# The second block's first half: the context as a thread of its own, woven between the latents' stages, its weights streamed twice

## The reference, cut to what matters

```
for i in (0, 1):                       # layer 0: MLA, layer 1: neighbourhood attention (NA)
    mod   = silu(c)     @ ada_w[i] + ada_b[i]     # shifts, scales, gates of the latents
    mod_c = silu(c_ctx) @ ada_w[i] + ada_b[i]     # and of the context
    h, hc = x * (1 + sc1) + sh1, ctx * (1 + csc1) + csh1
    y, yc = mixer(h, hc)               # latents attend to context and latents, the context to itself
    x   = layer_norm(alpha * x + g1 * y)
    ctx = layer_norm(alpha * ctx + cg1 * yc)             # layer 0 only
    x   = layer_norm(alpha * x + g2 * mlp(x * (1 + sc2) + sh2))
    ctx = layer_norm(alpha * ctx + cg2 * mlp(ctx * (1 + csc2) + csh2))   # layer 0 only
```

## Time and profile before

| | |
|---|---|
| median of the runs | 3009.98 us (3008.04 to 3012.18) |
| profiled execution, span | 3008.3 us |
| PE busy | 2883.5 us, 96% |
| PEld busy | 2401.1 us, 80% |
| DVE busy | 1953.4 us, 65% |
| ACT busy | 1152.3 us, 38% |
| POOL busy | 316.4 us, 11% |
| HBM read | 408.67 MB, 136 GB/s over the span |
| mean granted TensorE clock | 0.974 |

### The profile page before, as it was taken

How to read it: one execution, slowest core, us unless ns; L and a number is a source line. 1 busy time by engine, 2 the same in 40 slices (tenths; PEclk the granted TensorE clock), 3 DMA queues, 4 the chain that set the end, 5 groups by cost and what they waited for, 6 DMA issues and landing times.

```text
span 3008.3 us, 39317 instructions
## 1 busy us (share of the span) xinstructions
PE 2883.5 (96%) x15758; PEld 2401.1 (80%) x15758; DVE 1953.4 (65%) x3295; ACT 1152.3 (38%) x1901; POOL 316.4 (11%) x380
## 2 busy tenths in 40 slices
PE   7999999988999999999999899999999999998898
PEld 6888897546888888888887799976788888876898
DVE  7788855645688856778655765554566765457654
ACT  4222244443422224222254654434352223535553
POOL 0000011322100001000011120210230001200100
PEclk8999999979999999999999999999999999999999
DMA  6666522101455535555332245421134442343453
GB/s 239 222 218 227 186 86 88 42 28 42 154 204 202 203 105 175 198 201 209 114 124 73 68 161 183 147 84 36 64 118 161 169 147 92 92 103 79 130 186 119
DMA packets 126004, 412.27 MB, mean 137 GB/s; under 512 B 25296, under 2 KB 27472, under 8 KB 125312
## 3 DMA queue, kind: packets, MB, share of 16 engines
q1 hardware_dynamic: 110272, 353.14, 35.0%
q0 software_dynamic: 15552, 56.63, 5.3%
HBM read 408.67 MB, written 1.05 MB: 136 GB/s over the span
## 4 chain that ended last, share of the span: by engine, by line
PE 84%; DVE 6%; ACT 5%; issue 1%; DMA 1%; POOL 1%; SPq 0%; ACTq 0%; POOLq 0%; DVEq 0%
PE bank L2409 26%; PE bank L2410 25%; PE bank L2411 25%; PE bank L2678 2%; DVE sb_split_low L1829 1%; ACT sb_split_high L1415 1%; POOL sb_temp L1288 1%; DVE sb_h_low L1916 1%; DMA sb_na_raw<-na_rpb 1%; PE bank L2639 1%; DVE sb_temp L1910 1%; PE bank L2826 1%; PE bank L2761 0%; PE bank L2612 0%; DMA sb_raw<-weights 0%
## 5 line engine op out<-in xcount | busy, mean ns | idle before, releaser
L2409 PE MATMUL bank<-sb_h_high,sb_split_high 128*128 128x256 f32 (+1 forms) x3040 | 1050.3, 346 | 40.4 <-DVE sb_h_low L1924 18.7
L2410 PE MATMUL bank<-sb_h_low,sb_split_high 128*128 128x256 f32 (+1 forms) x3040 | 1030.2, 339 | 0.0
L2411 PE MATMUL bank<-sb_h_high,sb_split_low 128*128 128x256 f32 (+1 forms) x3040 | 1029.9, 339 | 0.0
L1829 DVE TENSOR_TENSOR sb_split_low<-sb_raw,sb_split_high 128x1024 fp32r<-128x1024 f32 x515 | 632.0, 1234 | 229.9 <-ACT sb_split_high L1415 227.2
L2409 PEld LDWEIGHTS bank<-sb_h_high,sb_split_high 128*128 128x128 f32 x3040 | 581.6, 191 | 128.6 <-DVE sb_h_low L1924 19.9
L1415 ACT ACTIVATE sb_split_high<-sb_raw 128x1024 fp32r<-128x1024 f32 x515 | 536.5, 1051 | 322.4 <-DMA sb_raw<-weights 322.2
L2411 PEld LDWEIGHTS bank<-sb_h_high,sb_split_low 128*128 128x128 f32 x3040 | 582.3, 192 | 64.7
L2410 PEld LDWEIGHTS bank<-sb_h_low,sb_split_high 128*128 128x128 f32 x3040 | 582.9, 192 | 63.7 <-issue 0.5
L1843 DVE CUSTOM_DVE_ANT_0 sb_temp<-sb_ada_ffn,sb_cond_ffn 128x1024 bf16<-128x1024 f32 x396 | 465.9, 1220 | 16.9 <-DMA sb_ada_ffn<-ada 8.5
L2032 DVE SCALAR_TENSOR_TENSOR sb_x_res<-bank,sb_gates,sb_x_res 128x256 f32<-128x256 f32 x320 | 145.1, 480 | 231.0 <-PE bank L2411 224.2
L2409 PE MATMUL bank<-sb_hidden_high_ffn,sb_split_high 128*128 128x512 f32 (+1 forms) x830 | 279.6, 337 | 0.0
(11 more groups left out here) (291 smaller groups left out, 3046.1 us busy)
## 6 DMA issues: line engine op xcount, KB each, us to landing
sb_raw<-weights SPq DMA_DIRECT2D x515, 512.0 KB, 3.3
sb_ada_ffn<-ada SPq DMA_DIRECT2D x114, 512.0 KB, 4.4
sb_ada_ffn<-ada POOLq DMA_DIRECT2D x90, 512.0 KB, 3.7
sb_ada_mlp<-ada POOLq DMA_DIRECT2D x18, 512.0 KB, 3.5
sb_ada_mlp<-ada SPq DMA_DIRECT2D x18, 512.0 KB, 4.3
sb_cond_ffn<-cond SPq DMA_DIRECT2D x3, 1024.0 KB, 5.1
sb_na_raw<-na_rpb SPq DMA_DIRECT2D x32, 96.0 KB, 6.0
sb_x_res<-tokens SPq DMA_DIRECT2D x4, 512.0 KB, 7.4
```

What stands on the lines that cost most here:

```text
L1829: do.tensor_tensor(m.low[i][:, :], m.raw[i][:, :], m.high[i][:, :].bitcast(F32), ALU.subtract).then_inc(*dve.mark("split_low", s))
L2409: do.matmul(out, ah, bh, start=start and j == 0, stop=False)
L2410: do.matmul(out, ah, bl, start=False, stop=False)
L2411: last = do.matmul(out, al, bh, start=False, stop=stop and j == len(terms) - 1)
```

## The change

The context's layer 0 and its keys and values for layer 1 get steps, slabs and signals of their own, with a `c` ahead of the name (`cmla_down`, `cmla_out`, `cmlp0`, `cna_k`, `cna_v0`, ...). The latents' ones become `LAT_PART`. The 105 slabs that both need are laid in the stream twice, each where it is used (`PLACE`, worked out from the order of the `done` steps). All the products of this half have 256 columns, but those of `mla_v` and `na_v`, whose moving side is the weights.

- `beside_ffn11`: the context's whole attention (down-projection, front, 8 units, out-projection, layer norm `cln00`) in banks 0 to 3, the pieces of the latents' `ffn11` between them in banks 4 and 5; the rest of `ffn11` follows.
- `beside_mla`: the latents' final norm, MLA and layer norm `ln00`, with the 64 pieces of the context's perceptron `cmlp0` between them; the rest of `cmlp0` follows.
- `beside_mlp0`: the latents' `mlp0` with the 36 rows of modulation, the context's second norm `cln01` woven into its first eight pieces and the tiles `cp10` into its last five; then the latents' norm `ln01` with the pieces of `cna_k` and `cna_v` between its groups.
- `na_steps` begins with the latents' `na_k` and `na_q` in turns of one slab each; five slabs of each lie beside the units, two in a turn, then `na_v1`.
- The warm matmuls of these norms are left out (those of `n12` and of the last half of `odd_out` stay). `ffn11` is cut in chunks of 8, 7, 7 instead of 22. The scores of layer 1 are two matmuls of 256 keys. SBUF is laid out anew; scales, gates and two temporaries exist twice.

The diff, cut to its core:

```diff
-          ("mla_down", 7), ("mla_uk0", 1), ("mla_v0", 1), ("mla_pe", 2), ("mla_uq0", 2),
-          ("mla_uq2", 2), ("mla_uk1", 1), ("mla_v1", 1), ("mla_out", 8), ("mlp0", 64),
-          ("na_k", 8), ("na_q", 5), ("na_v0", 4), ("na_q5", 3), ("na_v1", 4), ("na_out", 8), ("mlp1", 64)]
+          *((c + name, n) for c in ("c", "") for name, n in (
+              ("mla_down", 7), ("mla_uk0", 1), ("mla_v0", 1), ("mla_pe", 2), ("mla_uq0", 4), ("mla_uk1", 1), ("mla_v1", 1),
+              ("mla_out", 8), ("mlp0", 64), ("na_k", 8), ("na_v0", 4), ("na_v1", 4))),
+          ("na_q", 8), ("na_out", 8), ("mlp1", 64)]
...
-    "mlp0": ("relu2", 204, 36, BOTH),
+    "cmlp0": ("relu2", 0, 0, CTX_PART),
+    "mlp0": ("relu2", 204, 36, LAT_PART),
...
+def filled(groups, fill, n=1):
+
+    for group in groups:
+        yield from group
+        for _ in range(n):
+            if fill:
+                yield from fill.pop(0)
...
+def mla_front(p, ring, fill):
+
+    kv, q = of(p, "mla_kv"), of(p, "mla_q")
     square, add = (lambda tag, k: ("small_square", tag, k)), (lambda tag, k: ("small_sum", tag, k))
...
+    groups = [[square(kv, 0), square(kv, 1)],
+              [add(kv, 0), add(kv, 1), square(q, 0), square(q, 1), ("mean", kv, p)],
+              [add(q, 0), add(q, 1), square(q, 2), square(q, 3)],
+              [("mla_norm", kv, 0), ("mla_norm", kv, 1)] + [("rope", "mla_k", 0, 7)] * (p == LAT_PART),
+              [add(q, 2), add(q, 3), ("mean", q, p)]]
+    yield from filled(groups, fill)
...
+def mla_units(p):
+
+    return list(pair_turns(of(p, "mla"), 8, 2))
...
+def beside_ffn11():
+
+    ring = Ring(0, 6)
+    tiles = plain_tiles("cp00", 0)
+    early = in_groups([t for t in tiles if t[0] == "plain" or t[2] < 4], (1,) * 11)
+    late = [t for t in tiles if t[0] != "plain" and t[2] >= 4]
+    first, *rest = [out_piece("odd_out", k, 1, LAT_PART, ring) for k in range(DT)]
+    yield from weave([kept_warm(first, 8), *rest], early)
+    down = [fm_piece("cmla_down", j, CTX_PART, ring) for j in range(7)]
+    norm = ada_norm_groups("n12", 1)
+    yield from norm[0]
+    yield from late
+    yield from down[0]
+    yield from weave(norm[1:], down[1:4])
+    yield "gates", "ffn11"
+    _, body, _ = ffn_pieces("ffn11", Ring(4, 2), 0, 0)
+    ring = Ring(0, 4)
+    yield from filled([[], *down[4:]], body)
+    yield from mla_front(CTX_PART, ring, body)
+    ring = Ring(4, 2)
+    own = mla_own(CTX_PART, Ring(0, 4))
+    yield from flat(own)
+    yield from beside(mla_units(CTX_PART), body)
+    yield "gates", "cmla_out"
+    ring = Ring(0, 4)
+    outs = [out_piece("cmla_out", k, half, CTX_PART, ring) for half in (0, 1) for k in range(DT)]
+    yield from weave(outs, [body.pop(0) for _ in range(8)])
+    yield "scales", "cp01"
+    yield from filled(layer_and_plain_groups("cln00", "cp01", 0), body)
+    yield from flat(body)
...
+def beside_mla():
+
+    _, fill, _ = ffn_pieces("cmlp0", Ring(4, 2), 0, 0)
+    ring = Ring(0, 4)
+    yield "gates", "cmlp0"
+    yield "scales", "p00"
+    yield from filled([[("sum", "final", 1), ("mean", "final", 1)], [("rstd_spread", "final", 1), ("final_norm",)]], fill)
+    yield from filled(in_groups(plain_tiles("p00", 1), (4,)), fill)
+    yield from flat(fm_piece("mla_down", j, LAT_PART, ring) for j in range(7))
+    yield "gates", "mla_out"
+    yield from mla_front(LAT_PART, ring, fill)
+    own = mla_own(LAT_PART, Ring(0, 4))
+    yield from flat(own)
+    yield from beside(mla_units(LAT_PART), fill)
+    ring = Ring(0, 4)
+    outs = [out_piece("mla_out", k, half, LAT_PART, ring) for half in (0, 1) for k in range(DT)]
+    yield "cond", "mlp0", 1
+    yield from weave(outs, [fill.pop(0) for _ in range(4)])
+    yield "scales", "p01"
+    yield from filled(layer_and_plain_groups("ln00", "p01", 1), fill, 2)
+    yield "cond_silu", "mlp0"
+    yield from flat(fill)
...
+def beside_mlp0():
+
+    yield "gates", "mlp0"
+    ring = Ring(0, 6)
+    _, body, _ = ffn_pieces("mlp0", ring, 0, 0)
+    pieces = list(ada_pieces("mlp0", body))
+    yield from weave(pieces[:8], [[], [], *layer_norm_groups("cln01", 0)])
+    yield from flat(pieces[8:-5])
+    yield "scales", "cp10"
+    yield "scales", "p10"
+    yield from weave(pieces[-5:], in_groups(plain_tiles("cp10", 0), (5, 5, 5, 5)))
+    ring = Ring(0, 6)
+    yield "na_bv",
+    yield "na_rpb", 0
+    names = [fm_piece("cna_k", j, CTX_PART, ring) for j in range(8)] + [piece for g in (0, 1) for piece in tm_pieces(f"cna_v{g}", ring)]
+    yield from filled(layer_and_plain_groups("ln01", "p10", 1), names, 2)
+    yield "gates", "na_out"
+    yield from flat(names)
...
         if k == 0:
             return
+        if tag == "cln01":
+            pool.wait_ge("turned", ("mla", 7, 1))
```

More of the change, by code:

```diff
@@ L958, in schedule, with places @@
+def places():
+    order_of = [step[1] for step in order() if step[0] == "done"]
+    assert sorted(order_of) == list(range(N_SLABS))
+    at = [0] * N_SLABS
+    for i, s in enumerate(order_of):
+        at[s] = i
+    return at
+PLACE = places()
 def schedule():
@@ L2504, in small_sum @@
         pe.wait_ge("squared", (tag, k))
-        do.matmul(m.bank[bank][:, 0:n], m.C("ones"), m.squares[k % 2][:, 0:n], start=k == 0, stop=k == tiles - 1).then_inc(
+        do.matmul(m.bank[bank][:, 0:NC_TOK], m.C("ones"), m.squares[k % 2][:, cols], start=k == 0, stop=k == tiles - 1).then_inc(
             *pe.mark("summed", (tag, k)))
@@ L2541, in out @@
         if halves:
[L2542 removed]
+            s, first = PLACE[SLAB0[name] + 4 * half + k // 2], halves[half]
             free(bank)
@@ L2827, in mla_scores @@
-        for c in range(2):
-            bank, rows = (2 * u + c) % 3, slice(HD * c, HD * c + HD)
-            do.matmul(m.bank[bank][:, 0:n], big[rows, MLA_QPE + pair, qs], big[rows, MLA_KPE, 0:n], start=False, stop=True).then_inc(
-                *pe.mark("scored", ("mla", u, c)))
-            read[bank] = "exped", ("mla", u, c)
+        pair_of_scores("mla", u)
     def na_scores(u):
```

572 lines of the change are left out of this document (321 added, 251 removed), and 2 rows, old and new, of the table GATES.

## The result

The changed kernel takes 3091.06 us (median of 4 runs, 3089.63 to 3095.13) against 3010.28 us before (4 runs beside it). The ratio is 1.0269, with a 95% interval of 1.0257 to 1.0281: 81 us slower. The forecast was 3005 us, range 2978 to 3032. It had the wrong sign, and the time lies 59 us above the range.

What follows compares the result with a forecast made beforehand. TensorE, busy 2883.5 of 3008.3 us, was taken as the bound, so only its waits or slowness could be won. Terms 7 + 2 - 47 + 5 - 8 + 32 + 4 = -5 gave 3005 us, range 2978 to 3032.

Steps and rivals of the forecast that it cites:

- the -47 around the norms: Around the norms: TensorE's 73 us of gaps would be filled except 26 us of remaining waits, winning 47 us.
- the -8 of the second attention: Second attention: ten slabs' products of na_k and na_q as filler would cut TensorE's idle time, winning 8 us.
- The width, +7: Products split from 512 columns into two of 256 would cost 7 us more in all.
- "VectorE needs ... a step of 4.11": mlp0, +32: Latents' mlp0: VectorE's steps, up to 4.11 us, outlast TensorE's slabs, so it takes 212 us, not 180: 32 us more.
- Rival B: Latents' mlp0: VectorE's load decides, TensorE waits 50 us instead of 32; 3030 us in all, slower; chance 0.20.
- the 36 stay: Latents' mlp0: the 36 modulation rows VectorE works out remain beside it though the context's half leaves; within the +32 us.
- "Attention", first one, +5: First attention: waits from head pairs sharing bank 6, now four pairs each for context and latents, would add 5 us.
- two together in a turn: Second attention: a slab each of na_k and na_q beside one turn gives 5.6 us of filler; within the -8 us.
- "Coupling", +4: Two threads sharing in-order queues hold each other's operations back, mostly hidden by TensorE's five-slab lead: 4 us more.
- Rival C: Latents' mlp0: the holes bring TensorE's clock down, 24 us on top, 3029 us, slower; chance 0.04.
- Rival D: Gaps are only moved: other waits in the context's thread hold TensorE as long, time within 0.2%; chance 0.09.

Runs made afterwards that it cites:

- mlp0 by parts: The kernel before, with each 512-column product of mlp0 made as two of 256 from the same slab: 3016.24 us, ratio 1.0015.
- cln01 bare: The changed kernel with no piece of the other stream between the norms' and fronts' groups or the out-projections' pieces: 3109.43 us, ratio 1.0329.
- the norm spread out: The changed kernel with the context's norm cln01 spread between pieces 5 to 18 of mlp0: 3087.08 us, ratio 1.0256.
- a piece ahead of the first sums: The changed kernel with filler ahead of the first sums of cln00, final, ln00, ln01, and two pieces behind each p00 group: 3076.04 us, ratio 1.0220.
- all four causes out: The changed kernel with mlp0's 72 dot products cut to 64 columns, cln01 spread out, filler before first sums, na_k ahead of the second attention: 3028.90 us.
- One slab a turn: The changed kernel with all eight slabs of the latents' na_k ahead of the second attention's units: 3076.44 us, ratio 1.0222.
- short dot products: The changed kernel with VectorE's 72 dot products beside mlp0 cut to 64 of 1024 columns (output wrong): 3057.14 us, ratio 1.0160.
- four edits together: The changed kernel with 14 modulation rows beside cmlp0, filler before first sums, cln01 spread out, na_k ahead of the second attention: 3079.15 us, ratio 1.0225.

## Why the prediction was wrong

The forecast's sum was -5 us and the measured span +82. Of the 87 us between them some 34 lie in the second attention, 28 before mlp0, 22 in mlp0 and 3 at ln01. Two steps gave the forecast its sign, and both failed: the -47 around the norms was mis-sized, and the -8 of the second attention had the wrong sign.

**The width, +7.** Right where it was tested: the kernel before with mlp0 by parts costs 4.5 us, and this term has 4.7 for it.

**"VectorE needs ... a step of 4.11": mlp0, +32.** The mechanism was right and the term too small: 234 us, not 212. With cln01 bare mlp0 takes 214.4 us, of which the forecast without the norm was about 204. The norm was priced at 8 us of VectorE's time; woven, it costs 234.1 - 214.4 = 20. Its chain of sum, root and spread crosses POOL, ScalarE and a VectorE queue that is already late, so TensorE waited 9.5 and 7.7 us for it (or, with the norm spread out, 11.6 more for hidden_low). Rival B, with its sign and its point of decision (over 220 to 225 us), described this stretch; I gave it 0.20, and its 3030 us was still 61 short, since it too had the other stretches wrong.

**"the 36 stay": their loads.** The prediction halved the slab time for VectorE's work but not for the lead of the modulation loads. By the order a load is issued about one piece ahead of its use, so it had 5.6 us to land and now has 2.8, while landing takes 5.0 us (median). In the changed kernel this costs 3 us or nothing; it is what kept the lighter versions from being faster (23 us).

**"What is won around the norms", -47.** Mis-sized. About 32 of the 47 belonged to the stretch before mlp0 and 15 to ln01.

At ln01 it came: the part ahead of the second attention went from 101.2 to 78.2 us. It holds 384 products of 256 and 168 of 512 columns before, 339 and 143 after. Less these at the prediction's spacings of 0.117 and 0.230 us and its 2.1 us for the sums, 15.6 us were lost there before and 3.5 are now, against the 4 that the forecast left (an estimate, as its own were). The one wait of TensorE there is ln01's first sum, 2.3 us.

The stretch before mlp0 missed its forecast by 28 us, and this is where the step failed; between the woven and the unwoven kernel there lie only 10.6 us there. I took the whole gap, slow clock and warm matmuls included, as winnable, and left 22 us of waits here. TensorE has 52, of them 8 in the first attention. What is left in place of the gaps are short waits of either stream on three engines. That a piece ahead of the first sums wins 7 us there and 5 at ln01 shows that a part is plain distance. The remainder in the first half (23 us up to mlp0's end with all four causes out, some 7 of it width and 5 the first attention) is not settled; that the eviction queues of the two streams hold each other up is argued, not shown.

**"Attention", first one, +5.** Right: its waits for bank 6 went from 3.1 us to 5.0 + 2.7.

**"Attention", second one, -8.** Wrong in sign. Less its products (49 of 256 and 96 of 512 columns before, 241 and 50 after) the attention up to na_out takes 49.7 us before and 69.2 after, and 7 us more lie behind the cut: some 26 us more, not 8 less. The failed step is "two together in a turn": I counted their products as filler and VectorE's time per turn, but not that the filler has two banks. Two products a turn fill both, and the next one waits for copies that stand in VectorE's and ScalarE's queues behind the turn's own work. One slab a turn wins 15 us. What the rest comes from is not settled; waits of 8.2 us for copies of na_q remain there.

**"Coupling", +4.** Far too small. It was added at the end as a remainder, and at cln01 and in the second attention it is the subject: there, by what ended its waits, TensorE waited for work that stood in an in-order queue behind another thread's.

**Rival C, the clock.** The clock did fall (0.91 in mlp0). Before mlp0 it gave no time back when filler raised it. In mlp0 it rose to 0.96 when VectorE's load fell, so it came with the waits; 10 of the 32 us won there are matmuls at a faster clock, and how much of that TensorE could have used with the waits in place is not shown. **Rival D** had 0.09 and was near the truth in the stretch before mlp0, where most of the holes only moved; at ln01 they went, and for the whole it is wrong.

## What to carry to other kernels

When a stage's pieces are halved, go through everything that is laid out in pieces rather than in microseconds: side work on another engine, the lead of each load, the distance between the links of a norm. The dot products here were hidden by 5.6 us a slab and were not by 2.8, and relieving one of these can bring little until the next is relieved too: rows moved away brought nothing until their loads were issued earlier. Count the banks and the queue of the engine that frees them before putting two fillers where one was.

## What was not expected

The transfers did not limit mlp0 by their rate: with the four causes out it reads 269 GB/s with the DMA engines 0.76 busy, and no wait of TensorE there is put down to a load. Their time to land did grow. A modulation load took 4.3 us from SP and 3.5 from POOL before (medians), and 5.0 and 5.1 after the change. In the kernel with short dot products that shows as 16 waits of VectorE, up to 5.6 us each. They cost little there, since VectorE had time to spare (TensorE waited 0.8 us for hidden_low); in the version with four edits together, issuing them earlier won 23 us.
